# 32 of 256 tokens leave the dense expert matrices for gathered rows, and both expert phases stream two halves past one weight load

## The reference

```python
q = (xb @ w_query).reshape(PEER_TOKEN_BLOCK, PEER_HEADS, 2, D_KEY // 2)
s = jnp.einsum('thpc,pkc->thpk', q, sub_keys).astype(jnp.float32)
...
u = expert_u[e]
act = jax.nn.gelu(jnp.einsum('td,thkd->thk', xb, u).astype(jnp.float32))
return jnp.einsum('thk,thkd->td', (g * act).astype(xb.dtype), expert_v[e])
```

## Time and profile before

| what | value |
|---|---|
| median of 3 runs | 1251.67 us (1251.4 to 1252.78) |
| the profiled execution's own time | 1253.08 us |
| its span | 1251.2 us |
| PE busy | 1238.5 us, 99% of the span |
| DVE, ACT, POOL busy | 940.7, 689.3, 34.3 us |
| DMA moved | 261.61 MB, mean 209 GB/s |
| granted TensorE clock | 0.999 of full |

### The profile page before, as it was taken

How to read it: one execution, slowest core, us unless ns; L and a number is a source line. 1 busy time by engine, 2 the same in 40 slices (tenths; PEclk the granted TensorE clock), 3 DMA queues, 4 the chain that set the end, 5 groups by cost and what they waited for, 6 DMA issues and landing times.

```text
span 1251.2 us, 21981 instructions
## 1 busy us (share of the span) xinstructions
PE 1238.5 (99%) x8585; PEld 1127.5 (90%) x8585; DVE 940.7 (75%) x1706; ACT 689.3 (55%) x1153; POOL 34.3 (3%) x29
## 2 busy tenths in 40 slices
...
GB/s 280 205 145 135 153 177 205 199 193 194 194 150 247 135 116 209 156 250 249 242 237 245 219 225 186 220 202 190 244 256 274 229 245 234 236 247 252 243 251 95
DMA packets 73127, 261.61 MB, mean 209 GB/s; under 512 B 8320, under 2 KB 8832, under 8 KB 72768
## 3 DMA queue, kind: packets, MB, share of 16 engines
...
q10 hardware_dynamic: 432, 0.56, 0.1%
...
## 4 chain that ended last, share of the span: by engine, by line
PE 90%; DVE 4%; DMA 2%; ACT 2%; issue 1%; SPq 0%; DVEq 0%; ACTq 0%
PE ps L1189 27%; PE ps L557 15%; PE ps L558 14%; PE ps L559 14%; PE ps L549 13%; PE ps L1152 2%; DVE wlo L1742 1%; PE ps L594 1%; DMA raw<-in_w_in_a_dram 1%; ACT whi L1232 1%; PE ps L607 1%; DVE turned_x L2081 1%; PE ps L1111 1%; DMA raw<-in_w_in_dram 1%; PE ps L624 1%
## 5 line engine op out<-in xcount | busy, mean ns | idle before, releaser
L1232 ACT ACTIVATE whi<-raw 128x1024 fp32r<-128x1024 f32 (+2 forms) x420 | 441.7, 1053 | 453.5 <-PE ps L559 199.9
L1742 DVE TENSOR_TENSOR wlo<-raw,whi 128x1024 fp32r<-128x1024 f32 (+2 forms) x409 | 495.6, 1215 | 232.8 <-ACT whi L1232 230.0
L557 PE MATMUL ps<-turned_x,whi 128*128 128x256 f32 x1504 | 419.0, 279 | 0.0
L558 PE MATMUL ps<-turned_x,whi 128*128 128x256 f32 x1504 | 416.0, 277 | 0.0
L559 PE MATMUL ps<-turned_x,wlo 128*128 128x256 f32 x1504 | 415.9, 277 | 0.0
L1189 PE MATMUL ps<-whi,turned_x 128*128 128x512 f32 x1024 | 315.6, 389 | 0.0
L557 PEld LDWEIGHTS ps<-turned_x,whi 128*128 128x128 f32 x1504 | 282.6, 188 | 0.7 <-issue 0.5
L558 PEld LDWEIGHTS ps<-turned_x,whi 128*128 128x128 f32 x1504 | 282.8, 188 | 0.0
L559 PEld LDWEIGHTS ps<-turned_x,wlo 128*128 128x128 f32 x1504 | 282.4, 188 | 0.0
L1189 PEld LDWEIGHTS ps<-whi,turned_x 128*128 128x128 f32 x1024 | 192.2, 188 | 39.9
L1189 PE MATMUL ps<-wlo,turned_x 128*128 128x512 f32 x512 | 199.2, 389 | 0.0
...
## 6 DMA issues: line engine op xcount, KB each, us to landing
raw<-in_expert_u_dram SPq DMA_DIRECT2D x128, 512.0 KB, 4.4
raw<-in_expert_v_dram SPq DMA_DIRECT2D x128, 512.0 KB, 5.0
raw<-in_w_up_dram SPq DMA_DIRECT2D x32, 512.0 KB, 4.2
raw<-in_w_down_dram SPq DMA_DIRECT2D x32, 512.0 KB, 3.7
acts<-stage SPq DMA_DIRECT2D x32, 512.0 KB, 3.0
stage<-acts SPq DMA_DIRECT2D x30, 512.0 KB, 3.3
raw<-in_w_in_dram SPq DMA_DIRECT2D x20, 512.0 KB, 4.1
raw<-in_w_gate_dram SPq DMA_DIRECT2D x16, 512.0 KB, 3.5
```

What stands on the lines that cost most here:

```text
L557: e.matmul(dst, whi[:, h, sl], xh[:, k, :], start=k == 0, stop=False)
L558: e.matmul(dst, whi[:, h, sl], xl[:, k, :], start=False, stop=False)
L1232: e.activation(whi[:, u % NH, 0:n], raw[:, u % NR, 0:n], ACT.Copy).then_inc(*hi(u))
L1742: e.tensor_tensor(wlo[:, u % NH, 0:n], raw[:, u % NR, 0:n], whi[:, u % NH, 0:n].bitcast(F32), ALU.subtract).then_inc(*lo(u))
```

## The change

- The dense path keeps 224 tokens (DENSE); the last 32 leave it. All tiles with a token axis become 224 wide, the groups of one-hot tiles go from 64 to 56.
- In both phases one matmul streams the big and the small part of the tokens (2 x 224 columns, two pieces of `turned_x`) past one load of whi; a second one streams 224 columns past wlo. Big x big plus big x small thus lie in the two halves of a bank.
- In the u phase ScalarE copies the second half out of PSUM (`take_low_u`) and TensorE adds it to the first by a matmul with an identity (`join`, 224 columns), one unit later. The gelu comes after that.
- In the v phase the roles of the operands are exchanged: the stationary operand is a 128-column piece of the expert rows, and eight banks hold the sums with channels on partitions. At the end ScalarE and VectorE add the halves, TensorE turns them back (`turn_end`), and the closing norm is done for both token halves together.
- The 32 tokens have 32 x 128 chosen experts, which are 32 steps for 128 partitions. GpSimd gathers 128 rows of `expert_u` in each of 32 indirect DMAs and 128 rows of `expert_v` in each of 32 more, 512 KB each, into a ring of three (`fetch_rows`). VectorE makes a dot product of each of the first 32 (`tensor_tensor_reduce`, 1024 elements) and a scaled sum of each of the others. They are spread: one every second unit in the u phase from EU+58, one every 3.25 units in the v phase.
- Routing is compressed: UB1 1.75 for 1.35, TURN_AT 53 for 67, one-hots from 55 for 69. 16 units between EU+4 and EU+49 have their subtraction on GpSimd.

The core of the diff:

```diff
+DENSE = 224
+GROUPS = DENSE // 4
-UB1 = 1.35
+UB1 = 1.75
...
-LO_POOL = (BR_B + 1, BR_B + 2, BR_B + 3, OUT, OUT + 1, UP, UP + 1, IN2, IN2 + 1, QUERY, QUERY + 1)
+LO_POOL = (BR_B + 1, BR_B + 2, BR_B + 3, OUT, OUT + 1, UP, UP + 1, IN2, IN2 + 1, QUERY, QUERY + 1,
+           *range(EU + 4, EU + 50, 3))
-EXP_AT, TURN_AT, HOT_FROM = 45, 67, 69
+EXP_AT, TURN_AT, HOT_FROM = 36, 53, 55
...
+            def join(n):
+                e.wait_ge(*lows_a.at(n))
...
+                e.matmul(ps[u_bank(n)][:, 0:DENSE], unit_r[:, :], lows[:, :], start=False, stop=True,
+                         skip_group_check=True).then_inc(*summed(n))
...
-                m = cols(EU + n, 0, 8, TH, TL, ps[b][:, 0:256], range(4))
...
+                for k in range(8):
+                    h, sl = (EU + n) % NH, slice(k * 128, k * 128 + 128)
+                    e.matmul(ps[b][:, 0:2 * DENSE].rearrange("p (w t) -> p w t", w=2), whi[:, h, sl], THL[:, :, k, 0:DENSE],
+                             start=k == 0, stop=False)
+                    m = e.matmul(ps[b][:, 0:DENSE], wlo[:, h, sl], TH[:, k, 0:DENSE], start=False, stop=k == 7)
...
+            def accumulate(n, c):
+                h, sl = (EV + n) % NH, slice(c * 128, c * 128 + 128)
+                e.matmul(ps[c][:, 0:2 * DENSE].rearrange("p (w t) -> p w t", w=2), whi[:, h, sl], THL[:, :, n % 8, 0:DENSE],
+                         start=n == 0, stop=False)
+                return e.matmul(ps[c][:, 0:DENSE], wlo[:, h, sl], TH[:, n % 8, 0:DENSE], start=False, stop=n == 127)
...
+            for c in range(7):
+                take_low(c)
+            e.wait_ge(*lo.at(UNITS - 1))
+            end_squares(0, 0, 6)
+            take_low(7)
+            end_squares(1, 6, 7)
+            end_squares(2, 7, 8)
...
+def rows_from(r):
+
+    return EU + 58 + 2 * r if r < 32 else EV + 2 + 13 * (r - 32) // 4
...
+            def fetch_rows(r):
+                e.wait_ge(*hi.at(rows_from(r)))
+                if r > 2:
+                    e.wait_ge(*row_d.at(f"dot{r - 3}" if r < 35 else f"sum{r - 35}"))
```

More of the change, by code:

```diff
@@ L401, in build @@
         d_out = [landing(f"out{i}") for i in range(4)]
+        d_rkept, d_listed, d_gated, d_at, d_gate, d_gain, d_shares, d_four = (
+            landing(n) for n in ("rkept", "listed", "gated", "at", "gate", "gain", "shares", "four"))
+        d_held, d_scale = landing("held", range(4)), landing("scale", range(4))
+        d_rows = [landing(f"rows{i}", range(i, 64, 3)) for i in range(3)]
         used = signal("used", range(EV + 125))
@@ L527, in build @@
         end_d = signal("end_d", (
-            "x00 x01 v0 g00 g01 r0 out01 x10 g10 x11 v1 g11 r1 out11").split())
+            "zero rows0 rows1 rows2 rows3 c0 c1 c2 c3 x0 x1 x2 x3 c4 c5 x4 c6 x5 c7 x6 tot v x7 g0 g1 r out01 out11").split())
+        row_d = signal("row_d", [*(f"dot{r}" for r in range(32)), "act", *(f"sum{r}" for r in range(32))])
+        row_p = signal("row_p", [
+            "x", "gain", "g00", "g10", "g01", "g11"])
         def tensor_program(e):
@@ L1182, in tensor_program, with turn_end @@
                         m.then_inc(*turned(f"route{i}"))
-            def accumulate(n, t, d):
-                h, sl = (EV + n) % NH, slice(t * 128, t * 128 + 128)
-                for k, (x, w) in enumerate(((RH, whi), (RH, wlo), (RL, whi))):
-                    m = e.matmul(ps[bank4(t, d)][:, :], x[:, n % 8, sl], w[:, h, d * 512:d * 512 + 512],
-                                 start=n == 0 and k == 0, stop=n == 127 and k == 2)
-                return m
+            def accumulate(n, c):
[3 more added lines that the diff above has]
+                return e.matmul(ps[c][:, 0:DENSE], wlo[:, h, sl], TH[:, n % 8, 0:DENSE], start=False, stop=n == 127)
+            def turn_end(c):
+                e.wait_ge(*end_d.at(f"c{c}"))
+                for t in range(2):
+                    m = e.transpose(ps[c][:, t * 128:t * 128 + 128], sums4[:, c, t * 128:t * 128 + 128], ident)
+                m.then_inc(*turned(f"end{c}"))
             for n in range(125):
@@ L2514, in vector_program @@
                     split(EU + n + 2)
+                row_products(EU + n)
                 if n == TURN_AT:
@@ new lines, in end_sums @@
+            def end_sums(c):
+                e.wait_ge(*turned.at(f"end{c}"))
+                xs = X[:, :, 128 * c:128 * c + 128]
+                e.tensor_tensor(xs, xs, ps[c][:, 0:256].rearrange("p (t n) -> p t n", t=2), ALU.add).then_inc(*end_d(f"x{c}"))
+            e.wait_ge(*d_gb4.at(0))
+            take_sums(0)
+            take_sums(1)
+            take_sums(2)
+            take_sums(3)
+            for c in range(4):
+                end_sums(c)
+            take_sums(4)
+            take_sums(5)
@@ new lines, in vector_program @@
+            for t in range(2):
+                e.tensor_tensor(fin[:, t, 768:1024], X[:, t, 768:1024], gb4[:, 768:1024], ALU.mult).then_inc(*end_d(f"g{t}"))
+            e.wait_ge(*end_a.at("s1"))
+            e.reciprocal(end_r, end_s).then_inc(*end_d("r"))
+            e.wait_ge(*end_d.at("r"))
+            e.wait_ge(*end_d.at("g1"))
+            for t in range(2):
+                e.wait_ge(*row_p.at(f"g{t}1"))
+                scaled_copy(fin[:, t, 512:1024], fin[:, t, 512:1024], end_r[:, t:t + 1]).then_inc(*end_d(f"out{t}1"))
```

305 lines of the change are left out of this document (213 added, 92 removed), and 1 row of the table turned.

## The result

The changed kernel takes **1275.95 us** (median of 4 runs, 1272.79 to 1285.31) against 1252.22 beside it on the same chip: ratio 1.020, 95% interval 1.015 to 1.026, so slower by 24 us where 34 less were forecast. The profiled execution took 1274.55, its span is 1272.7 us. On its page TensorE (PE) is no longer full and GpSimd (POOL) has work.

The account below looks back on a forecast made before the run. TensorE was taken to bound the kernel, busy to the last hundredth, with VectorE next. Terms -13.5 - 3.6 - 27.7 + 1.5 + 1 + 2.5 + 5.5 = -34.3 us gave 1217.4 against 1251.67, range 1194 to 1242.

Parts of the forecast that it names:

- The pair: Both phases: one 448-column and one 224-column matmul per piece, forecast at 0.313 us together (0.297 to 0.322).
- terms 1 and 3: TensorE's matrix work: u phase 2.614 us a unit with join, -13.5 us; v phase 2.504 a unit, -27.7 us.
- terms 2 and 5: Gates: 56 groups for 64, -3.6 us; seam between phases: waits for last gelus and ScalarE copies, +1 us.
- term 7: Tail after the last matmul: longer chain of squares, copies and adds before the last store, +5.5 us (4 to 7).
- term 6: Both phases: VectorE close behind TensorE, so an uneven unit can be late, +2.5 us (0 to 8).
- rival B: VectorE becomes the bound, held back by GpSimd's 16 subtractions: about 1234 us, chance 0.17.
- Rivals A and D: A: pair only 0.297 us, 1193 us, chance 0.12; D: shared load saves nothing, pair 0.337 us, 1267 us, chance 0.04.
- Rival C: Gather stretches: added gathers make the DMA the bound; landings of 9.5 us in the v phase give 1263 us, chance 0.10.

Follow-up runs that it names:

- e2: Changed kernel with GpSimd's 16 subtractions cut to 32 of 2048 columns each: 1265.9 us.
- e14: e2 plus, behind each thin subtraction, a GpSimd subtraction of 128x1024 that nobody waits for: 1276.0 us.
- e12: Changed kernel with load ahead of fetch (v phase), store one load later and three 224-column matmuls without join (u phase): 1242.7 us.
- e15: e12 with no u unit subtracted on GpSimd, routing spread over 64 units, and one-hots and gathers later: 1228.7 us.
- e1: Changed kernel without the 64 gathers of expert rows and the waits for them; VectorE's row operations still run: 1251.7 us.
- e5: Changed kernel with SyncE issuing each v unit's load before the fetch of the gelus instead of behind it: 1253.2 us.
- e3: Changed kernel without VectorE's 64 row operations and the gelu of the dots, gathers kept: 1268.1 us.
- e10: Changed kernel with SyncE issuing each u-phase store of gelus one load later: 1266.5 us.
- e18: e15 with the pairs of 448 and 224 columns and the join in the u phase again: 1227.1 us.

## Why the prediction was wrong

- **The pair, terms 1 and 3:** right. 0.313 forecast, 0.316 to 0.318 measured; by the unit (2.64 for 2.614, 2.53 for 2.504) that is 3.3 us in each phase. Rivals A and D fall. The Trainium skill's formula ("TensorE: Matmul & The Clock Gate", Back-to-back issue gap) gives an estimate of 0.189 us for 448 columns. This case's rows have 0.21 to 0.22.
- **The gates and the seam, terms 2 and 5:** right. Four groups take 1.77 us (1.80), and before the join at the seam PE is idle for 0.18 us, so the seam costs less than the 1 us forecast.
- **The tail, term 7:** +5.5 forecast (4 to 7). It is 7.0 - 2.85 = 4.1 from the last matmul's end to the last store's issue, and 4.7 by the spans. Within its range.
- **Jitter, term 6 (+2.5, 0 to 8):** mis-sized through rival B, which was given 0.17. I argued that GpSimd's subtractions fall beside searches with one input and that three units of lead cover them. They met VectorE's own subtractions often enough to make the mean 1610 ns. Worked out there as 16 us, it is 10 (e2, e14) and at most 14.6 (e12 to e15, with the new spread of the routing). The rule of the Trainium skill ("SBUF — State Buffer", Who interferes with whom) that the two exclude each other for whole instructions agrees with e14's 4.40 and 3.26 us; it deserved more than the 0.5 us of the earlier trace rows, which showed only the tail of one meeting.
- **Rival C, the step that failed.** It counted the circle of a slot as landing, ScalarE and VectorE, 5.0 + 1.06 + 1.22, and found room up to landings of 7.7 us. It left out the time from a free slot to the issue of its load; the sum has no term for it, so it went in as nothing, without a reason. In the v phase SyncE's load stands, at every fourth unit, behind a fetch, which waits for VectorE's `take`: 3.45 us in the kernel before, and I had never read that queue. With it 0.9 us of the 10.9 were left for these loads, and units that are shorter by 0.8 us in four use them up. The gathers' traffic then had no room left: late loads reach ScalarE 4.8 us after their issue where it is 4.3 without gathers (e1, medians). Late issue and the place behind the fetch cost 26 us in the v phase, and the load ahead of the fetch gave them back (e5). The DMA did not become the bound (e5: 0.86 busy, 0.2 us of idle PE, landings of 6.2, within the 7.7); the order in SyncE's queue did.
- **Row operations:** priced as VectorE's time only (2.39 of 2.50 us a unit). That time did fit. That `take`, the fetch and two loads stand behind the row operation was not asked; e3, where the first of the two is 2.4 us late instead of 3.6, shows 7.5 us in v.
- **The join:** priced as a weight load, with the remark that PE now waits for ScalarE within one unit. It also made the gelu one unit later, and SyncE's store waits for the gelu, with the loads behind it, 5.1 us late where it had been 2.3: 7 to 10 us (e10). I named the first and missed the second.
- Sum of the singles: e5 -23, e10 -9.5, GpSimd -10 to -14.6 make 1229 to 1233 of 1276; e18 has 1227.1. Of the remaining 10 us to the forecast of 1217, 6.7 are the pair's (256 x 0.026); the rest is not traced.

That the gathers cost the v phase 20 us (e1) and that the order costs it 26 (e5) are both true. In the new order the gathers cost nothing (0.2 us of idle PE), and without the gathers the old order costs 6 (331.5 against 325.8); the other 20 need both. It was shown by taking each away.
